# Earlier places in three queues: modulation tiles, a conv loop's product sums, a norm's centring and a table load

## The chip, the cores and the metric

The kernel runs on one core of a Trainium2 chip. A core has TensorE (matmuls; PE in the profile, its weight loads PEld), VectorE (DVE), ScalarE (ACT), GpSimd (POOL) and SyncE (SP), which here issues nearly all DMAs. Each engine works through its own queue in order, and engines wait for each other by semaphores. Three of the names below are memories: SBUF, which all engines read and write, PSUM, where TensorE accumulates and which VectorE and ScalarE read and write too, and HBM, where inputs and weights lie. The metric is device time in microseconds (us).

## The reference, cut to what matters

Three model blocks in a row on one sequence of 512 tokens with 1024 features, all in float32. The change touches the start of the first block and the middle of the second:

```python
# first block: six modulation vectors from a condition c of 1024 values
mod = silu(c) @ ada_w + ada_b                      # 1024 x 6144
sh_m, sc_m, g_m, sh_f, sc_f, g_f = split(mod, 6)
h = rms_norm(x, mix_norm_g) * (1.0 + sc_m) + sh_m  # wants the first 2048 columns of mod
proj = h @ w_in                                    # dq, dk, dv, sq, sk, sv, then attention
...
# second block, conv module: 2048 channels, 31 taps
a, b, z = split(h @ w_in, 3)
u = a * sigmoid(b)
c = causal_depthwise_conv(u, dw_w) + dw_b          # 31 multiply-adds for each channel
mu, var = mean(c), mean((c - mu) ** 2)             # over the 2048 channels
cn = (c - mu) * rsqrt(var + EPS) * ln_g + ln_b
y = silu(cn) * silu(z)
x = x + y @ w_out                                  # conv_out
...
# after it, retention: q and k are turned by angles positions * inv_freq
```

## The kernel before

Activations lie transposed: a chunk is 128 features on the partitions by 512 tokens. `st.X` holds the 8 chunks of x, `st.A` 32 chunks of work space, `st.spare` 16 more; `Hh`, `Hl` and `Bh`, `Bl` hold the high and low part of the 8 chunks that the next matmuls read. To keep float32's accuracy each product is made of three: high by high, high by low, low by high (line 1329).

**The weight stream** (`weights_part`). Weights come in tiles of 1024 rows by 256 columns (1 MB), alternately into the two slots of `st.raw`. SP loads a tile when GpSimd has split the tile before the last (lines 1215 to 1222); GpSimd splits it into `Wh` (line 1276) and `Wl` (line 1282, four instructions) once TensorE is through with the tile before the last; TensorE multiplies it in 48 matmuls, into one of two accumulators of two PSUM banks each; VectorE or ScalarE takes the result. The list that `program` makes fixes the order on each engine: segments of tiles, and between them parts with their own programs. A part's SP program stands in SP's queue between the loads of the segment ahead and those of the segment behind. A segment can carry `beside` (more work for GpSimd behind a tile's split) and `after` (more for VectorE behind a tile).

**The modulation** (`modulation_parts`). `ada_w` is cut in 24 tiles like the weights. The first 8 give the shift and gain that the first norm wants. SP loads them in turn into four slots: two are the two of `st.raw`, two lie in `st.spare`; tile n+4 waits until tile n is used. VectorE multiplies seven of them by silu(c) and adds them up over the rows in 8 instructions (lines 482 and 484), TensorE adds the partitions (line 458); tile 3 (`BY_PE`) TensorE multiplies itself, in 16 matmuls (line 469). The first two tiles of `w_in` can only be loaded when `raw` is free again. The other 16 tiles go through `st.spare` beside the projections. Before the third tile of `w_in`, SP issues 11 small loads (`beside_weights`: lambdas, head parameters, `skip` in single elements).

**The conv module** (`conv_module_steps`). Eight pairs of channel chunks, three weight tiles for each: sigmoid of b (ScalarE), the gated product (`glu`, VectorE, lines 2771 to 2774), silu of z (ScalarE). Of the 31 taps VectorE does 23, 46 multiply-adds a pair (line 2805); ScalarE starts the sums with two (line 2762) and makes the products of six more (line 2767), and GpSimd adds these six up: `add_half` adds the first three behind one split and the others behind the next (line 2791). It waits for the semaphore `products`, which ScalarE raises once for a pair, behind the sixth.

**The norm of the conv module** (`conv_norm_parts`, "norm5"). It centres in two steps. TensorE sums chunks 0 to 9 (line 2861), ScalarE makes their mean, the pivot, in `st.spare` (line 2890). The pivot is subtracted from 16 chunks: the first 5 by GpSimd (`BY_POOL`, line 2884), the last two and 5 to 13 by VectorE (line 2943). ScalarE squares each (line 2898), TensorE adds the squares up (line 2871) and finds the rest of the mean from chunks 10 to 15 (lines 2866 and 2876). VectorE makes variance (lines 2945 to 2955), then for chunks 0 to 7 subtracts the remaining offset (line 2957), scales (2925), multiplies by the gate `times` (2929; chunks 16 to 31 of `A`) and makes the low part (2933), with ScalarE's silu and high part between. Chunks 8 to 15 follow in groups of 3, 3 and 2 behind the first three tiles of the next segment (`second_half`, line 2973). `norm5.ready(k)` says that chunk k's low part is done.

**What follows.** The list reads `conv_in, norm5, rescaled(), conv_out[0], tables, conv_out[1]`: `conv_out[0]` multiplies norm chunks 0 to 7 with four weight tiles, `conv_out[1]` chunks 8 to 15 with four more. `tables` (`rotary_parts`) makes the rotary angles: SP waits for `memory_free`, then loads the positions into chunk 16 of `A` (line 1824); VectorE works on them in chunks 17 and 18. GpSimd's part of the norm sits in `behind_first_tile`: behind the split of `conv_out[0]`'s first tile the first additions of the last pair, behind the second tile's the other additions and the centring.

## Time and profile before

| | |
|---|---|
| median of 3 runs | 2705.58 us (2704.51 to 2707.02) |
| profiled execution | 2704.16 us, of which the span of the trace is 2702.0 us |
| granted TensorE clock, mean over the span | 0.968 of full |
| TensorE busy | 2530.6 us (94%) |
| GpSimd busy | 1542.3 us (57%) |
| VectorE busy | 1405.9 us (52%) |
| ScalarE busy | 646.8 us (24%) |
| HBM read | 227.86 MB, 85 GB/s over the span |

The span runs from the first to the last record; the 2.2 us beside it lie around it. Busy time leaves out waiting, and semaphore and DMA-issuing instructions. Two levels of TensorE's clock occur, 1.2 and 2.4 GHz, which the windows show as 0.50 and 1.00. In the time line, "x3" stands for three instructions in a row with their whole length, and the brackets give the engine's idle time before the first and what ended it. An engine's name with a q (SPq, POOLq) is its queue: issuing, waiting, draining.

### The profile page before, as it was taken

The page shows a single profiled execution, that of the slowest core. Times are in us where ns is not written, and L with a number is a line of the kernel's source. Part 1 is how long each engine was busy: PE and PEld are TensorE (multiplying, and loading weights), DVE is VectorE, ACT ScalarE, POOL GpSimd, SP SyncE. Part 2 cuts the span into 40 slices and gives each one's busy share as a digit, 9 for nine tenths or more (in the row PEclk, how much of TensorE's full clock was granted, in tenths as well). Part 3 has the DMA queues.
Part 4 walks back from the last instruction along what each step waited for, and adds up shares of the span by engine and source line. Part 5 has one row for each costly group of instructions (what it writes and reads, how often), then busy time and mean ns, then how long its engine had stood idle before and what let it go on. Part 6 is the DMA issues. An engine that isn't in the chain of part 4 may idle for free.

```text
span 2702.0 us, 32177 instructions
## 1 busy us (share of the span) xinstructions
PE 2530.6 (94%) x11690; PEld 2019.7 (75%) x11690; DVE 1405.9 (52%) x1944; ACT 646.8 (24%) x1045; POOL 1542.3 (57%) x1039
## 2 busy tenths in 40 slices
PE   6998999999989997699999998998998998999997
PEld 4885678888777774578977885866887786878775
DVE  6886552221489998848214336243356134535354
ACT  3106630110353343321022114132113212100001
POOL 2640266766688886267633754525762665666552
PEclk8999999999999999899999999999999999999998
DMA  8650022223322221122220222312331222223221
GB/s 268 217 164 1 32 78 94 93 94 94 102 71 78 92 83 56 35 94 94 93 78 32 98 91 62 94 33 63 94 94 32 78 93 78 78 93 93 93 72 42
DMA packets 231014, 231.36 MB, mean 86 GB/s; under 512 B 10011, under 2 KB 228860, under 8 KB 230780
## 3 DMA queue, kind: packets, MB, share of 16 engines
q1 hardware_dynamic: 228368, 228.87, 26.6%
q8 instruction: 63, 1.03, 0.2%
q10 hardware_dynamic: 2540, 1.11, 0.2%
q14 instruction: 43, 0.35, 0.0%
HBM read 227.86 MB, written 2.10 MB: 85 GB/s over the span
## 4 chain that ended last, share of the span: by engine, by line
PE 79%; DVE 7%; ACT 3%; DVEq 3%; POOLq 3%; issue 1%; DMA 1%; POOL 1%; ACTq 0%; SPq 0%
PE PS L1329 67%; PE PS L1185 2%; POOLq L2794 2%; PE PS L1902 1%; POOLq L1278 1%; PE PS L930 1%; POOL Wl L1282 1%; DMA raw<-in_ada_w 1%; DVE PS L2805 1%; PE PS L2104 1%; ACT spare L2767 1%; PE PS L2121 1%; PE PS L2871 1%; PE PS L1893 1%; DVEq L2700 0%
## 5 line engine op out<-in xcount | busy, mean ns | idle before, releaser
L1282 POOL TENSOR_TENSOR Wl<-raw,Wh 128x512 fp32r<-128x512 f32 (+2 forms) x768 | 1049.4, 1397 | 28.8 <-issue 7.3
L1276 POOL TENSOR_SCALAR Wh<-raw 128x2048 fp32r<-128x2048 f32 (+2 forms) x196 | 366.9, 1873 | 932.9 <-PE PS L1329 495.6
L1329 PE MATMUL PS<-Hh,Wh 128*128 128x512 f32 (+1 forms) x1976 | 784.6, 397 | 68.6 <-POOL Wl L1282 23.3
L1329 PE MATMUL PS<-Hl,Wh 128*128 128x512 f32 (+1 forms) x1976 | 778.2, 394 | 0.0
L1329 PE MATMUL PS<-Hh,Wl 128*128 128x512 f32 (+1 forms) x1976 | 778.0, 394 | 0.0
L1329 PEld LDWEIGHTS PS<-Hh,Wh 128*128 128x128 f32 (+1 forms) x1976 | 375.2, 190 | 164.5 <-issue 50.6
L1329 PEld LDWEIGHTS PS<-Hh,Wl 128*128 128x128 f32 (+1 forms) x1976 | 374.7, 190 | 81.7 <-issue 1.0
L1329 PEld LDWEIGHTS PS<-Hl,Wh 128*128 128x128 f32 (+1 forms) x1976 | 375.6, 190 | 78.9 <-issue 0.7
L1329 PE MATMUL PS<-Bh,Wh 128*128 128x512 f32 x688 | 272.4, 396 | 27.2 <-POOL Wl L1282 18.4
L1329 PE MATMUL PS<-Bl,Wh 128*128 128x512 f32 x688 | 270.9, 394 | 0.0
L1329 PE MATMUL PS<-Bh,Wl 128*128 128x512 f32 x688 | 270.9, 394 | 0.0
L2805 DVE SCALAR_TENSOR_TENSOR PS<-spare,PS 128x512 f32<-128x512 f32 x368 | 251.8, 750 | 9.8 <-ACT PS L2762 2.2
L1329 PEld LDWEIGHTS PS<-Bh,Wh 128*128 128x128 f32 x688 | 131.1, 191 | 59.3 <-POOL Wl L1282 18.9
L1329 PEld LDWEIGHTS PS<-Bh,Wl 128*128 128x128 f32 x688 | 131.0, 190 | 27.6
L1329 PEld LDWEIGHTS PS<-Bl,Wh 128*128 128x128 f32 x688 | 131.2, 191 | 27.1
L1329 PE MATMUL PS<-Wh,Hh 128*128 128x256 f32 x512 | 145.1, 283 | 0.0
L1329 PE MATMUL PS<-Wh,Hl 128*128 128x256 f32 x512 | 144.9, 283 | 0.0
L1329 PE MATMUL PS<-Wl,Hh 128*128 128x256 f32 x512 | 144.9, 283 | 0.0
L1413 DVE SCALAR_TENSOR_TENSOR X<-X,PS 128x512 f32<-128x512 f32 (+1 forms) x64 | 41.1, 682 | 194.9 <-PE PS L1329 194.9
L2695 DVE TENSOR_SCALAR A<-PS,params 128x512 f32 (+1 forms) x68 | 47.9, 745 | 143.8 <-PE PS L1329 143.4
L2697 DVE SCALAR_TENSOR_TENSOR A<-PS,params,A 128x510 f32 (+5 forms) x160 | 112.4, 744 | 14.7 <-issue 13.5
L1329 PEld LDWEIGHTS PS<-Wh,Hl 128*128 128x128 f32 x512 | 98.3, 192 | 0.1
(458 smaller groups left out, 2899.4 us busy)
## 6 DMA issues: line engine op xcount, KB each, us to landing
raw<-in_w_in SPq DMA_DIRECT2D x44, 1024.0 KB, 5.8
raw<-in_w_ff SPq DMA_DIRECT2D x32, 1024.0 KB, 5.3
raw<-in_conv_w_in SPq DMA_DIRECT2D x24, 1024.0 KB, 5.2
raw<-in_ret_w_in SPq DMA_DIRECT2D x24, 1024.0 KB, 5.1
spare<-in_ada_w SPq DMA_DIRECT2D x20, 1024.0 KB, 7.2
raw<-in_w_up SPq DMA_DIRECT2D x20, 1024.0 KB, 5.4
raw<-in_w_out SPq DMA_DIRECT2D x8, 1024.0 KB, 5.0
raw<-in_conv_w_out SPq DMA_DIRECT2D x8, 1024.0 KB, 4.9
```

The costliest lines, as they stand in the source:

```text
L930: pe.matmul(self.SUMSQ, ones, self.sq[c % 4], start=(c == 0 and not self.pre), stop=(c == KC - 1)).then_inc(self.summed, 1)
L1185: mm = pe.matmul(acc_of(0)[0:m, b, :], w[:, k, b * P:b * P + m], x[:, k, :], start=(k == 0 and n == 0), stop=(k == KC - 1 and n == 2))
L1276: pool.tensor_scalar(st.Wh[0:rows, slot, k, 0:g.width], st.raw_slot(slot)[0:rows, k, 0:g.width], 1.0, 1.0, ALU.mult, ALU.mult)
L1278: pool.drain()
L1282: ins = pool.tensor_tensor(st.Wl[0:rows, slot, k, 0:g.width], st.raw_slot(slot)[0:rows, k, 0:g.width], st.Wh[0:rows, slot, k, 0:g.width].b ...
L1329: mm = pe.matmul(out, lhs, rhs, start=(k == parts[0][0] and n == 0), stop=(k == parts[-1][0] and n == 2))
L1413: ins = e.scalar_tensor_tensor(x, x, x_scale, a, ALU.mult, ALU.add)
L1893: mm = pe.matmul(st.PS[:, n % 2, 0:S - b * P], st.A[:, 8 + 2 * h + d, b * P:(b + 1) * P], st.A[:, 2 * h + d, b * P:S], start=(d == 0), sto ...
L2695: ins = e.tensor_scalar(out[0:m, b, :], acc[0:m, b, :], w, None, ALU.mult)
L2697: ins = e.scalar_tensor_tensor(out[0:m, b, back:S], acc[0:m, b, 0:S - back], w, out[0:m, b, back:S], ALU.mult, ALU.add)
L2794: e.drain()
L2805: e.scalar_tensor_tensor(s, U[:, b, k:k + S], wts[:, k, b:b + 1], s, ALU.mult, ALU.add)
```

## The change

Four edits.

1. **Modulation.** All eight first tiles get buffers of their own: tiles 0 to 3 the four slots in `st.spare`, tiles 4 to 7 `before_h`, a new name for the memory of `Hh` and `Hl`, which the first norm fills later. SP issues all eight without a wait in between, and `raw` is free for `w_in` from the start. TensorE multiplies tiles 3 and 7 itself, VectorE the six others.
2. **Products.** ScalarE raises `products` behind each of the six; `add_half` waits for three before its first half and for six before its second.
3. **Norm.** GpSimd centres ten chunks instead of five, and does all its work for the norm and the last pair behind the split of `conv_out[0]`'s first tile. VectorE centres six. ScalarE writes the pivot twice, for GpSimd in `st.spare` and for VectorE in PSUM; offset, rstd and mean square move from `st.spare` to PSUM banks 3 to 6.
4. **Tables.** SP's load of the positions waits for `norm5.ready(2)` instead of `norm5.ready(15)`.

```diff
@@ modulation_parts
-    SLOT = lambda s: st.raw_slot(s) if s < 2 else LATER_SLOT(s - 2)
+    SLOT = lambda n: LATER_SLOT(n) if n < N else \
+        st.before_h[:, 4 * (n - N):4 * (n - N) + 4, :].rearrange("p c (h n) -> p (c h) n", h=2)
-    N, BY_PE = 4, 3
+    N, BY_PE = 4, (3, 7)
-    rounds, by_dve = first // N, [n for n in range(first) if n != BY_PE]
+    rounds, by_dve = 1, [n for n in range(first) if n not in BY_PE]
...
-        for n in range(first):
-            load(sp, SLOT(n % N), n % N, n // N, n * TW)
-        sp.wait_ge(free[0], rounds + 1)
-
-    def second_slot_free(sp):
-        sp.wait_ge(free[1], rounds + 1)
+        for n in range(N):
+            load(sp, SLOT(n), n, 0, n * TW)
+        for n in range(N, first):
+            sp.dma_start(SLOT(n), w[:, :, ds(n * TW, TW)]).then_inc(landed_h[n - N], 16)
...
-        for k in range(1, len(by_dve)):
-            mm = add_up(k)
-        mm.then_inc(by_pe, 1)
+        for k in range(1, len(by_dve) - 1):
+            add_up(k)
+        pe.wait_ge(landed_h[BY_PE[1] - N], 16)
+        product(BY_PE[1])
+        add_up(len(by_dve) - 1).then_inc(by_pe, 1)
@@ conv_module_steps
             for b in range(2):
                 ins = e.activation(PROD[k][:, b, :], U[:, b, k:k + S], ACT.Copy, scale=wts[:, k, b:b + 1])
-        ins.then_inc(products, 1)
+            ins.then_inc(products, 1)
...
     def add_half(e, pair, half):
+        e.wait_ge(products, pair * BESIDE + (half + 1) * (BESIDE // 2))
         if half == 0:
-            e.wait_ge(products, pair + 1)
             e.sem_inc(going, 1)
@@ conv_norm_parts
-    EARLY, BY_POOL, HALF, RING = 10, 5, 8, 5
+    EARLY, BY_POOL, HALF, RING = 10, 10, 8, 5
...
-    pivot, offset, rstd = st.spare[:, 7, :], st.spare[:, 14, :], st.spare[:, 15, :]
-    square_mean, logs = st.spare[:, 13, :], st.spare[:, 12, :]
+    pivot, logs = st.spare[:, 7, :], st.spare[:, 12, :]
+    pivot_v, offset, rstd, square_mean = (st.PS[:, k, :] for k in range(3, 7))
+    rest, rest_sq = st.spare[:, 14, :], st.spare[:, 13, :]
...
         act.activation(pivot, TOTAL, ACT.Copy, scale=1.0 / (EARLY * P)).then_inc(pivot_in, 1)
+        act.activation(pivot_v, TOTAL, ACT.Copy, scale=1.0 / (EARLY * P)).then_inc(pivot_in, 1)
...
-            dve.tensor_tensor(src[c], src[c], pivot, ALU.subtract).then_inc(centred_v, 1)
-        dve.drain()
-        dve.tensor_scalar(offset, pivot, float(14 * P - EARLY * P) / width, None, ALU.mult)
+            dve.tensor_tensor(src[c], src[c], pivot_v, ALU.subtract).then_inc(centred_v, 1)
+        dve.tensor_scalar(rest, pivot_v, float(14 * P - EARLY * P) / width, None, ALU.mult)
...
-        dve.tensor_tensor(logs, offset, offset, ALU.mult)
+        dve.tensor_tensor(rest_sq, rest, rest, ALU.mult)
+        dve.tensor_copy(offset, rest)
...
         if (i, p) == (0, 0):
             conv_in.first_sums(pool)
-        if (i, p) == (0, 1):
             conv_in.last_sums(pool)
             centre_by_pivot(pool)
@@ program
+        st.before_h = nc.alloc_sbuf_tensor_at("before_h", [P, 2 * KC, S], F32, offset=before_h)
...
-                nc, st, t, norm5.ready(15), lambda c: queries.act_ready(c) if c < 8 else keys.act_ready(c - 8))
+                nc, st, t, norm5.ready(2), lambda c: queries.act_ready(c) if c < 8 else keys.act_ready(c - 8))
```

On GpSimd, from the last pair's last split on. Each `Wh` and `Wl` pair is one weight tile: the last of the conv module, then the first and second of `conv_out[0]`. Before:

```order
L1276 TENSOR_SCALAR Wh<-raw 128x2048
L1282 TENSOR_TENSOR Wl<-raw,Wh 128x512 x4
L2791 TENSOR_TENSOR spare<-spare 128x1024 x2
L1276 TENSOR_SCALAR Wh<-raw 128x2048
L1282 TENSOR_TENSOR Wl<-raw,Wh 128x512 x4
L2791 TENSOR_TENSOR spare<-spare 128x1024
L2791 TENSOR_TENSOR spare<-spare,extra 128x1024
L2791 TENSOR_TENSOR spare<-spare,A 128x1024
L2884 TENSOR_TENSOR A<-A,spare 128x512 x5
```

and after:

```order
L1283 TENSOR_SCALAR Wh<-raw 128x2048
L1289 TENSOR_TENSOR Wl<-raw,Wh 128x512 x4
L2798 TENSOR_TENSOR spare<-spare 128x1024 x3
L2798 TENSOR_TENSOR spare<-spare,extra 128x1024
L2798 TENSOR_TENSOR spare<-spare,A 128x1024
L2892 TENSOR_TENSOR A<-A,spare 128x512 x10
L1283 TENSOR_SCALAR Wh<-raw 128x2048
L1289 TENSOR_TENSOR Wl<-raw,Wh 128x512 x4
```

The five additions of products stand together, ten subtractions follow in place of five, and the second tile's split comes behind them all.

On VectorE, behind the conv of the last pair, up to the first three scalings of norm5. Before:

```order
L2943 TENSOR_TENSOR A<-A,spare 128x512 x11
L2945 TENSOR_SCALAR spare<-spare 128x512
L2948 SCALAR_TENSOR_TENSOR spare<-PS,spare 128x512
L2950 TENSOR_TENSOR spare<-spare 128x512
L2953 SCALAR_TENSOR_TENSOR spare<-PS,spare 128x512
L2955 TENSOR_TENSOR spare<-spare 128x512
L2957 TENSOR_TENSOR A<-A,spare 128x512 x8
L2925 SCALAR_TENSOR_TENSOR A<-A,params,spare 128x512 x3
```

and after:

```order
L2952 TENSOR_TENSOR A<-A,PS 128x512 x6
L2953 TENSOR_SCALAR spare<-PS 128x512
L2956 SCALAR_TENSOR_TENSOR spare<-PS,spare 128x512
L2958 TENSOR_TENSOR spare<-spare 128x512
L2959 COPY PS<-spare 128x512
L2962 SCALAR_TENSOR_TENSOR PS<-PS,spare 128x512
L2964 TENSOR_TENSOR PS<-PS,spare 128x512
L2966 TENSOR_TENSOR A<-A,PS 128x512 x8
L2934 SCALAR_TENSOR_TENSOR A<-A,params,PS 128x512 x3
```

Five subtractions are gone, one copy is new, and pivot, offset and rstd are read from PSUM (`PS`).

On TensorE at the start, behind the transposes of x: partition sums of VectorE's tiles (four matmuls a tile), squares of the first norm (128x512), and its own product of a tile (16 matmuls from `small`). Before:

```order
L458 MATMUL PS<-squares,A 128x1 x4
L667 MATMUL PS<-A,squares 128x512 x4
L469 MATMUL PS<-small,spare 128x1 x16
L667 MATMUL PS<-A,squares 128x512 x4
L458 MATMUL PS<-squares,A 128x1 x24
```

and after:

```order
L457 MATMUL PS<-squares,A 128x1 x4
L674 MATMUL PS<-A,squares 128x512 x4
L464 MATMUL PS<-small,spare 128x1 x16
L674 MATMUL PS<-A,squares 128x512 x4
L457 MATMUL PS<-squares,A 128x1 x16
L464 MATMUL PS<-small,before_h 128x1 x16
L457 MATMUL PS<-squares,A 128x1 x4
```

One tile's sums are gone, and a second product stands ahead of the last tile's sums.

## Rows read from the trace of the kernel before

**Rows 1.** The page, part 1: busy us (share of the span) xinstructions.

```profile
PE 2530.6 (94%) x11690; PEld 2019.7 (75%) x11690; DVE 1405.9 (52%) x1944; ACT 646.8 (24%) x1045; POOL 1542.3 (57%) x1039
```

**Rows 2.** Waits of TensorE, 735 to 1160 us: engine, line, releaser: total us, times, longest.

```profile
PE PS L1329 <- POOL Wl L1282: 40.5, 12, 18.4
PE PS L1329 <- DVE Hl L2933: 13.6, 1, 13.6
```

**Rows 3.** The same view for SP's queue, 1085 to 1210 us.

```profile
SPq L1824 <- DVE Bl L2933: 89.1, 1, 89.1
```

**Rows 4.** The chain that ended last, 1137 to 1160 us: start, us, what.

```profile
1137.12 0.34 SPq L1824
...
1137.57 7.55 DMA raw<-in_conv_w_out
```

**Rows 5.** Timeline of TensorE, 1153 to 1166 us: start, us, instruction [idle before <- releaser].

```profile
1153.43 0.80 PE L1329 MATMUL PS<-Bh,Wh 128*128 128x512 f32 x1 [18.44 <-POOL Wl L1282]
...
1158.57 0.39 PE L1329 MATMUL PS<-Bh,Wh 128*128 128x512 f32 x1
...
1165.86 0.39 PE L1329 MATMUL PS<-Bh,Wl 128*128 128x512 f32 x1
```

**Rows 6.** Timeline of VectorE, 1061 to 1132 us.

```profile
1061.12 6.74 DVE L2943 TENSOR_TENSOR A<-A,spare 128x512 f32<-128x512 f32 x11
...
1075.66 0.69 DVE L2953 SCALAR_TENSOR_TENSOR spare<-PS,spare 128x512 f32<-128x512 f32 x1 [5.37 <-PE PS L2871]
...
1103.88 4.52 DVE L2973 TENSOR_TENSOR A<-A,spare 128x512 f32<-128x512 f32 x3
...
1122.43 1.89 DVE L2973 TENSOR_TENSOR A<-A,spare 128x512 f32<-128x512 f32 x3
...
1130.01 1.28 DVE L1413 SCALAR_TENSOR_TENSOR X<-X,PS 128x512 f32<-128x512 f32 x2
```

**Rows 7.** Timeline of GpSimd, 1055 to 1112 us.

```profile
1055.11 6.18 POOL L2884 TENSOR_TENSOR A<-A,spare 128x512 f32<-128x512 f32 x5 [0.24 <-issue]
1102.55 1.92 POOL L1276 TENSOR_SCALAR Wh<-raw 128x2048 fp32r<-128x2048 f32 x1 [41.26 <-issue]
1104.61 6.65 POOL L1282 TENSOR_TENSOR Wl<-raw,Wh 128x512 fp32r<-128x512 f32 x4
```

**Rows 8.** The chain: the norm's sums, first matmuls of conv_out, and TensorE from 1206 us.

```profile
1065.32 10.31 PE PS L2871 x24
...
1089.23 13.14 PE PS L1329 x48
...
1206.23 175.15 PE PS L1329 x1134
```

**Rows 9.** Windows of 2 us: length, busy (x) by engine, granted clock, DMA share, GB/s.

```profile
1052.00:1054.00 2.00, 0.00 (x0) 0.00 (x0) 1.96 (x3) 0.00 (x0) 1.86 (x2) 1.00 0.00 1
...
1056.00:1058.00 2.00, 0.91 (x1) 0.50 (x2) 1.93 (x4) 1.00 (x2) 2.00 (x3) 0.50 0.00 0
```

**Rows 10.** Timeline of ScalarE: products of the last pair, and the pivot.

```profile
1027.76 5.01 ACT L2767 ACTIVATE spare<-spare 128x512 f32<-128x512 f32 x8
...
1046.95 0.60 ACT L2890 ACTIVATE spare<-PS 128x512 f32<-128x512 f32 x1 [6.18 <-PE PS L2861]
```

**Rows 11.** VectorE in the conv loop: its waits, and its 368 multiply-adds (ns min/median/max).

```profile
DVE spare L2771 <- PE PS L1329: 1.8, 3, 0.8
...
L2805 DVE SCALAR_TENSOR_TENSOR PS<-spare,PS x368: 746/750/758, 764.8 to 1057.5; 128x512 f32<-128x512 f32 x184
```

**Rows 12.** Waits of GpSimd, 735 to 1160 us.

```profile
POOL spare L2791 <- ACT A L2767: 20.5, 8, 3.4
```

**Rows 13.** The start: TensorE's wait, GpSimd's, and a window (columns above).

```profile
80.98 0.50 PE L1329 MATMUL PS<-Hh,Wh 128*128 128x512 f32 x1 [1.17 <-POOL Wl L1282]
...
73.13 2.09 POOL L1276 TENSOR_SCALAR Wh<-raw 128x2048 fp32r<-128x2048 f32 x1 [13.35 <-DMA raw<-in_w_in]
...
60.00:66.00 6.00, 5.55 (x25) 4.25 (x24) 5.38 (x11) 2.17 (x3) 0.00 (x0) 1.00 0.04 0
```

More of the change, by code:

```diff
@@ L460, in add_up, with product @@
             return mm
+        def product(n):
+            for b in range(2):
+                for k in range(KC):
+                    mm = pe.matmul(column(n, b), SLOT(n)[:, k, b * P:(b + 1) * P], silu_c[:, k:k + 1],
+                                   start=(k == 0), stop=(k == KC - 1))
+            return mm
         pe.wait_ge(c_act, 1)
@@ L2871, in square @@
             pe.matmul(SUMSQ, st.ones, ring[k % RING], start=(k == 0), stop=(k == n - 1)).then_inc(added, 1)
-        for k in range(BY_POOL - 1):
+        for k in range(BY_POOL):
             square(k)
@@ L2877, in _ @@
         mm.then_inc(rest_summed, 1)
-        for k in range(BY_POOL - 1, n):
+        for k in range(BY_POOL, n):
             square(k)
@@ L3131, in first_steps @@
                 seg.beside_load = lambda sp, i, p, at=at: [load_later(sp, n) for n in beside[at + p]]
-            dq.beside_load = lambda sp, i, p: mod_products.second_slot_free(sp) if p == 0 else [load_later(sp, n) for n in beside[1]]
             rope_tables, rope, rope_done = rope_parts(nc, st, t, slot_read)
```

39 lines of the change are left out of this document (20 added, 19 removed).

## The prediction

> **What bounds the kernel now.** The page's busy times come first: TensorE is busy for 94% of the span [rows 1], so a change is worth what it takes from TensorE's idle time or from its half-clock time, and work saved on another engine is worth nothing until TensorE waits for it. The next view is therefore who TensorE waits for. In the stretch that holds the conv module, its norm and the first half of `conv_out` (735 to 1160 us), it waits 40.5 us in 12 places for GpSimd's weight split and once 13.6 us for the norm's first low half [rows 2]. The largest single piece, 18.4 us, is the one to look at closest. SP's own waits name its origin: SP stood 89.1 us at line 1824 [rows 3], where it is to load the positions for the rotary tables but first waits for `norm5.ready(15)`, the last of the norm's sixteen chunks. SP works in order, and the next weight tile, the fifth of `conv_out`, is behind that wait. The chain shows what followed: SP gets free at 1137.12, the tile lands 7.55 us after it is asked for at 1137.57 [rows 4], GpSimd splits it, TensorE starts at 1153.43, 18.44 us after it had ended the fourth tile [rows 5], at 1134.99.
>
> **The positions' wait, `ready(15)` to `ready(2)`.** The positions and their tables go into chunks 16 to 18 of `A`, which are the gates of norm chunks 0 to 2 alone, so the new wait ends some 3 us after the first matmul of `conv_out`. I call the start of that matmul M; it is 1089.23 before [rows 8]. What is late next? Four conditions stand before the fifth tile's matmuls, which want to start at M+45.8 (1134.99 less 1089.23). (1) Its load needs the raw slot, free when the third tile is split: M+22.0 (1104.61 and 6.65) [rows 7]; landing 7.6 us later, M+29.5. (2) Its split needs the third tile's matmuls done, M+35 (45.8 less one tile of 10.9; a tile is 48 matmuls at 0.228 us, below), and takes 8.7 us, what the row of the contended third tile says (1102.55 to 1111.26) [rows 7]: M+43.6, so 2 us to spare. (3) The accumulator needs VectorE's addition of the third tile, at 1130.01 and 1.28 long [rows 6], M+42.1, 3.7 us to spare. (4) The norm's chunks 8 to 15: the last came at 1137.1, where SP's wait ended [rows 4], or M+48, but are wanted at the end of the tile, 8 us after its start. So the whole wait goes: **-18.4 us**.
>
> The wait also costs on the far side. After it the first twelve matmuls take 1153.43 to 1158.57, 5.14 us; the 32 from there to 1165.86 take 7.29, 0.228 each, and twelve of these are 2.73 us [rows 5]. TensorE came back at the lower level, 1.2 GHz, after standing still. Without the wait it doesn't stand: **-2.4 us**. Behind it the chain lies on TensorE's own matmuls, 1134 of them in a row from 1206 to 1381 us [rows 8], so nothing there takes the gain back. VectorE's nine table operations move from TensorE's idle time to the time of tile five and stretch beside GpSimd's split (three chunks took 4.52 us beside it against 1.89 without it [rows 6], 1.1 us extra each where contended). At 1.5 us each, as in that group, they end about M+63, the addition of tile five (M+56.7) is some 6 us late, and its accumulator is free at about M+64, wanted only at M+67.6: nothing.
>
> **The norm.** Before, GpSimd subtracts the pivot from 5 chunks in 6.18 us, behind five additions of products and the split of `conv_out`'s second tile [rows 7], and VectorE from the other 11 in 6.74, once its last conv is done at 1061.12; the sum of squares is then ready at 1075.66 [rows 6], 14.5 us on. TensorE is what runs in between: 1065.32 to 1075.63, 24 matmuls for 12 squares, 0.86 us a square [rows 8]. The new order does ten chunks on GpSimd, before that split: the pivot is there at 1047.55 [rows 10], and ten at 1.236 us end by 1059.9, before VectorE is free. ScalarE's and TensorE's share for these ten runs along with them (about 0.6 and 0.86 us, both under 1.24). From VectorE's start there remain 0.7 us for its first subtraction, then two chunks for the late total and six squares, eight times 0.86 or 6.9 us, and 0.1 for the handing over: 7.7 against 14.5, **-6.8 us**. VectorE's six subtractions (6 at 0.61, 3.7 us) and the four operations for the offset behind them (at the same 0.6 us, 2.4 and their drains) fit under TensorE's 7.7. The extra ScalarE copy of the pivot (0.6) lies under GpSimd's first subtraction. GpSimd's split of tile two now comes behind them and ends near 1068, with TensorE wanting it at M+13: some 27 us of cover; beyond them every us later would be a us of TensorE's. From the squares to M the same operations follow, 13.6 us (1075.63 to 1089.23).
>
> Their operands are in PSUM now. In the trace an operation with a PSUM operand steps as fast as one without: 1.28 us for two additions from PSUM, 0.60 apart, and 6.74 for eleven SBUF subtractions, 0.605 apart [rows 6]; I count nothing. The Trainium skill says otherwise ("VectorE: DVE Perf Modes", the section on the TRN2 errata): a VectorE operation costs 58 cycles on top of its elements from SBUF and 120 from PSUM, which at its 0.96 GHz is an estimate of 0.065 us more for each, 1.1 us over the some 17 on the path; by it the norm's term would be 5.7. This trace does not agree.
>
> In the second half of the norm the PSUM operands save VectorE time where GpSimd splits beside it, up to 2.6 us for a group of three [rows 6], and the earlier wish for tile five costs some back. It is VectorE's slack, not TensorE's: nothing.
>
> **The conv loop's products.** GpSimd waits 8 times, 20.5 us together, for ScalarE's sixth product, of which it first needs three [rows 12]; three products are six activations of 0.61 us, 3.7 us [rows 10], so the longest, 3.4, goes too. But GpSimd does not set the loop's length. VectorE runs its 46 multiply-adds of each pair back to back and waits for TensorE 3 times, 1.8 us together [rows 11]; that is what a GpSimd that is 2.6 us earlier for each pair can give. About 0.1 us of each wait is the signal's way: **-1.5 us**, with 0 and 1.8 as ends.
>
> **The first modulation.** One of seven tiles goes from VectorE to TensorE, whose product runs while VectorE does the others, all loads go out unasked, and the first matmul of `dq` can come some 1 to 2 us earlier. But two tiles later TensorE waits 1.17 us for the third weight tile, at 80.98, because GpSimd waited 13.35 us for its DMA until 73.13; and that DMA came late because the queue moved nothing from 60 to 66 us, working off SP's small scattered loads behind the megabytes [rows 13]. The bytes ahead of these are the same before and after, and the queues were full before too. TensorE gets to that wait earlier and waits longer: **0**, with ends of 1.2 us lost (an equal delay of that tile) and 2 us gained (all that the norm gains, should the tile come earlier too).
>
> **The sum** is 18.4 + 2.4 + 6.8 + 1.5 + 0 = 29.1 us off the profiled execution's 2704.16 us (span 2702.0 and 2.2 around it): 2675.1. The median of the runs is 1.4 us above that execution, so 2676.5 for the median. Its own range is 2673 to 2680.
>
> **Rivals.** (a) *TensorE sums at half clock.* Before, it stood still for 5.8 us; the clock was still full 2 us into that and at half when it resumed [rows 9]. The new order also ends ten squares early: if TensorE is through with `conv_in` sooner, the pivot comes sooner, and it may stand over 4 us before VectorE's two late chunks. The first 5 us or so of the eight sums then go at half speed, 2.6 us lost: 2679. For it: TensorE's slack in the loop; against: the ten squares keep it at work for 70% of the time up to then. 0.13. (b) *PSUM operands cost as in the skill's rule*; as a mechanism of this kernel, VectorE's path after the squares is 1.1 us longer: 2677.6, 0.04. (c) *The gap closes but for the split.* The 2 us to spare of condition 2 is small: if VectorE's rows hold GpSimd up more than in the third tile's split, TensorE waits 2 to 5 us: about 2680.5, 0.08. (d) *The change doesn't do what it says:* SP gets past the positions only late, for a reason that the rows don't show, and 20.8 us stay: 2697, 0.05. (e) *The start gives its 2 us too:* 2674.5, 0.05. (f) *Slower:* VectorE's 368 multiply-adds set the conv loop, and in the new order GpSimd's additions fall on other ones of them and on ScalarE's writes. If they got 0.079 us longer each (29.1 over 368), the gain would be gone; at 0.1 us it is 2713. Against it: beside GpSimd or not, all 368 took 0.746 to 0.758 us [rows 11]. 0.03. My forecast has 0.62.
>
> **How the numbers follow.** Predicted is the likeliest case, 2676.5. The range takes in its own range, (a), (b), (c) and (e) with the ends of the start's term: 2670 to 2685; (d) and (f) are left out with 0.08, and the rest of two tenths is for sizes that I misjudge. A measurement of this kernel can tell about 0.2%, 5.4 us, from no change: faster by more than that 0.95 (all but (f), and a part of (d)), within it 0.02, slower 0.03.
>
> **What would show it.** Right: SP's wait at the positions ends some 3 us after `conv_out` begins; TensorE has no wait between its fourth and fifth tiles, and the granted clock stays full there; from VectorE's last conv to the first matmul of `conv_out` 21 us instead of 28; GpSimd's wait for products gone and VectorE's waits for TensorE in the loop with it; a wait at the third weight tile at the start of 2 to 3 us, ending near 81 us. Wrong: a new wait of TensorE for GpSimd at the fifth tile; half clock in the norm's sums; subtractions with the pivot in PSUM that step above 0.65 us; multiply-adds of the conv above 0.70 us.

## The result, and the profile after

| | before | changed |
|---|---|---|
| median of 3 runs | 2705.58 us | 2685.93 us (2683.37 to 2687.91) |
| ratio to before | | 0.9926, 95% interval 0.9904 to 0.9949 |
| span of the profiled execution | 2702.0 us | 2684.1 us |
| granted clock, mean over the span | 0.968 | 0.969 |

The change makes the kernel 19.7 us faster. 29.1 had been forecast; the time lies 0.9 us above the upper end of the range. Two more groups of runs gave medians of 2682.52 and 2684.34 us for the same kernel, 22.4 and 18.8 us under before: both inside the range, and both well above the 2676.5 that was called likeliest.

The answers to [rows 2] and [rows 3] come first: the changed kernel's waits of TensorE and of SP's queue (engine, line, releaser: total us, times, longest), 735 to 1160 us.

```profile
PE PS L1336 <- POOL Wl L1289: 17.9, 7, 3.6
PE PS L1336 <- DVE Hl L2942: 13.6, 1, 13.6
PE PS L1336 <- issue: 4.1, 1, 4.1
PE PS L2884 <- DVE A L2952: 2.3, 1, 2.3
...
SPq L1831 <- DVE Hl L2942: 22.7, 1, 22.7
```

The wait of 18.4 us is gone, and SP waits 22.7 us for the norm instead of 89.1. The fourth row is new: TensorE stood 2.3 us for VectorE's first late chunk. The chain through the same place (start, us, what), for [rows 8]:

```profile
1061.75 3.55 PE PS L2884 x4
1065.29 5.30 PE PS L2879 x12
...
1084.13 93.82 PE PS L1336 x402
1177.95 2.58 PE PS L863 x6
1180.53 175.15 PE PS L1336 x1134
```

All eight tiles of `conv_out` are now in one piece of 402 matmuls. From its start, M, to the 1134 matmuls it is 96.4 us, before 117.0 (1206.23 less 1089.23): 20.6 us gained, for 20.8 forecast. VectorE's timeline through the norm, for [rows 6]:

```profile
1061.00 3.67 DVE L2952 TENSOR_TENSOR A<-A,PS 128x512 f32<-128x512 f32 x6
...
1070.62 0.70 DVE L2962 SCALAR_TENSOR_TENSOR PS<-PS,spare 128x512 f32<-128x512 f32 x1 [3.19 <-PE PS L2879]
...
1110.05 1.88 DVE L2982 TENSOR_TENSOR A<-A,PS 128x512 f32<-128x512 f32 x3
...
1119.51 1.28 DVE L1420 SCALAR_TENSOR_TENSOR X<-X,PS 128x512 f32<-128x512 f32 x2 [0.18 <-PE PS L1336]
```

From VectorE's start to M it is 23.1 us, before 28.1: 5.0 gained, for 6.8. The sum of squares came 9.6 us after the start instead of 7.7. Windows of the same place (length, busy us and instructions (x) of PE, PEld, DVE, ACT, POOL, granted clock, DMA share, GB/s) show why:

```profile
1060.00:1062.00 2.00, 0.25 (x1) 0.26 (x2) 1.91 (x3) 0.28 (x1) 2.00 (x2) 1.00 0.00 0
1062.00:1064.00 2.00, 2.00 (x3) 0.72 (x3) 2.00 (x4) 2.00 (x4) 2.00 (x3) 0.50 0.00 0
```

TensorE was through with the ten squares at 1059.4 and stood still; it came back at 1.2 GHz. In the conv loop the distance from 736 us to VectorE's last conv shrank by 3.0 us, for 1.5; VectorE's waits for TensorE are gone. Of GpSimd's 20.5 us for products 14.1 stay, in 6 waits of up to 2.5.

So the middle gained 28.6 us: at 736 us the changed kernel is 2.9 us behind before, at the 1134 matmuls 25.7 ahead (1206.23 less 1180.53). At the end it is only 17.9 ahead. **7.8 us are lost behind 1206 us, in code that the change does not touch.** One of the places, the first matmul of the third block's w_in and the chain piece that it begins, of before and then of the changed kernel:

```profile
1673.49 0.50 PE L1329 MATMUL PS<-Hh,Wh 128*128 128x512 f32 x1 [1.76 <-DVEq L1257]
...
1673.49 68.14 PE PS L1329 x480
```

```profile
1651.28 0.50 PE L1336 MATMUL PS<-Hh,Wh 128*128 128x512 f32 x1 [1.81 <-DVEq L1264]
...
1651.28 69.74 PE PS L1336 x480
...
1653.40 0.63 PE L1336 MATMUL PS<-Hl,Wh 128*128 128x512 f32 x1
```

The stand of TensorE is nearly the same, 1.76 and 1.81 us; before, the clock stays up behind it. In the changed kernel the matmuls step 0.43 us apart from 1652.6 to 1655.5 us, at 1.2 GHz, and the piece is 1.6 us longer. This place belongs less to the change than it seems: e4 and e16 below, which are the kernel before with a later start, have the longer piece too (69.76 and 69.74 us). At another place, the second block's retention, TensorE stood 2.6 us before and 3.0 after, behind a load of `decay` that was 0.5 us longer. The window behind the stand, of before and then of the changed kernel:

```profile
1389.00:1392.00 3.00, 2.62 (x11) 1.65 (x10) 0.71 (x2) 0.00 (x0) 0.00 (x0) 1.00 0.86 280
```

```profile
1363.00:1366.00 3.00, 2.79 (x8) 2.27 (x8) 1.04 (x3) 0.00 (x0) 0.00 (x0) 0.50 0.70 227
```

### The profile page after: what moved, and what is told of

Its sections match the earlier page's. It is cut to its first block, busy times and chain, and to the rows that moved or that the text cites. A ratio compares the mean times of both kernels' runs of the same rounds, so it can differ in the third digit from the quotient of the medians.

```text
span 2684.1 us, 32215 instructions
## 1 busy us (share of the span) xinstructions
PE 2538.7 (95%) x11714; PEld 2026.8 (76%) x11714; DVE 1394.6 (52%) x1932; ACT 647.5 (24%) x1046; POOL 1546.5 (58%) x1044
## 4 chain that ended last, share of the span: by engine, by line
PE 76%; DVE 12%; DVEq 5%; SPq 2%; ACT 2%; issue 1%; DMA 1%; ACTq 0%; POOLq 0%; POOL 0%
PE PS L1336 64%; DVE PS L2812 7%; DVEq L2814 2%; PE PS L1192 2%; PE PS L1909 1%; SPq L431 1%; PE PS L937 1%; PE PS L2111 1%; PE PS L2128 1%; PE PS L1900 1%; DMA raw<-in_w_in 1%; SPq L438 0%; DVEq L2707 0%; PE PS L2472 0%; PE PS L1553 0%
## 5 line engine op out<-in xcount | busy, mean ns | idle before, releaser
L1336 PE MATMUL PS<-Hh,Wh 128*128 128x512 f32 (+1 forms) x1976 | 784.3, 397 | 66.5 <-POOL Wl L1289 20.4
L1336 PEld LDWEIGHTS PS<-Bl,Wh 128*128 128x128 f32 x688 | 130.6, 190 | 26.9
L2704 DVE SCALAR_TENSOR_TENSOR A<-PS,params,A 128x510 f32 (+5 forms) x160 | 112.3, 743 | 14.8 <-issue 13.6
```

The costliest lines, as they stand in the source:

```text
L1336: mm = pe.matmul(out, lhs, rhs, start=(k == parts[0][0] and n == 0), stop=(k == parts[-1][0] and n == 2))
L2704: ins = e.scalar_tensor_tensor(out[0:m, b, back:S], acc[0:m, b, 0:S - back], w, out[0:m, b, back:S], ALU.mult, ALU.add)
```

## The experiments

All medians are in us. "Behind" is how much later than in the profiled execution of before the same piece of the chain starts (minus: earlier), at the third weight tile (81), `conv_in` (736), the 1134 matmuls (1206) and the end of the span. The clock is the mean over the executions of the run.

| run | median | before beside it | ratio, 95% interval | clock | behind at 81, 736, 1206, end |
|---|---|---|---|---|---|
| changed | 2685.93 | 2705.58 | 0.9904 to 0.9949 | 0.970 | 0.1, 2.9, -25.7, -17.9 |
| e1 wait's edit alone | 2689.84 | 2704.11 | 0.9930 to 0.9960 | 0.9710 | 0.2, 2.8, -10.6, -13.8 |
| e2 no modulation edit | 2678.88 | 2704.11 | 0.9884 to 0.9914 | 0.9728 | 0.2, 2.5, -25.2, -24.2 |
| e3 changed, 4 memsets | 2684.94 | 2704.11 | 0.9919 to 0.9946 | 0.9702 | 3.9, 7.7, -21.9, -18.9 |
| e4 before, 4 memsets | 2706.27 | 2704.11 | 0.9998 to 1.0017 | 0.9679 | 2.7, 6.0, 6.5, 3.7 |
| e5 changed, again | 2682.52 | 2704.88 | 0.9914 to 0.9938 | 0.9712 | 0.5, 1.7, -26.9, -26.2 |
| e6 no norm edit | 2694.28 | 2704.88 | 0.9954 to 0.9980 | 0.9684 | 0.0, 2.8, -14.3, -13.3 |
| e7 no products edit | 2681.67 | 2704.88 | 0.9906 to 0.9931 | 0.9713 | 0.3, 2.9, -22.3, -20.8 |
| e8 e2, small loads late | 2676.43 | 2704.88 | 0.9879 to 0.9910 | 0.9735 | -1.2, -1.1, -28.9, -24.8 |
| e9 changed, third time | 2684.34 | 2703.17 | 0.9908 to 0.9935 | 0.9708 | 0.3, 1.5, -27.1, -19.5 |
| e10 e2 again | 2678.52 | 2703.17 | 0.9893 to 0.9920 | 0.9722 | 0.2, 2.4, -25.2, -24.3 |
| e11 modulation edit alone | 2710.41 | 2703.17 | 1.0016 to 1.0034 | 0.9655 | 0.3, 1.8, 1.8, 5.5 |
| e12 changed, small loads late | 2682.41 | 2703.17 | 0.9911 to 0.9939 | 0.9706 | -2.2, -0.8, -29.2, -24.8 |
| e13 e11, tile 7 on VectorE | 2702.55 | 2704.32 | 0.9989 to 1.0006 | 0.9686 | 0.3, 0.2, 0.2, -3.5 |
| e14 e11, 4 memsets | 2715.12 | 2704.32 | 1.0022 to 1.0050 | 0.9658 | 3.4, 7.4, 8.0, 15.1 |
| e15 before, 2 memsets | 2707.49 | 2704.32 | 1.0002 to 1.0019 | 0.9672 | 1.4, 4.7, 5.5, 5.4 |
| e16 before, 8 memsets | 2709.76 | 2704.32 | 1.0013 to 1.0032 | 0.9682 | 5.4, 8.8, 9.0, 5.4 |
| e17 e13 and an extra product | 2707.21 | 2704.14 | 1.0003 to 1.0028 | 0.9667 | 2.8, 2.9, 3.0, 2.6 |
| e18 changed, tile 7 on VectorE, small loads late | 2676.80 | 2704.14 | 0.9880 to 0.9918 | 0.9712 | -0.9, 0.7, -27.6, -26.2 |

### The wait alone, and all without the norm or the products

e1 is before with one edit, e6 and e7 are the changed kernel with one edit undone. Of e6 and e7 one line each is shown.

```diff
-                nc, st, t, norm5.ready(15), ...     (e1: this and nothing else)
+                nc, st, t, norm5.ready(2), ...
-    EARLY, BY_POOL, HALF, RING = 10, 10, 8, 5       (e6: the norm's edit undone)
+    EARLY, BY_POOL, HALF, RING = 10, 5, 8, 5
-            ins.then_inc(products, 1)               (e7: the products' edit undone)
+        ins.then_inc(products, 1)
```

> The kernel before with the fourth edit alone: SP waits for norm chunk 2 instead of chunk 15 before it loads the positions. The profile of the changed kernel shows TensorE without a wait between the fourth and fifth tiles of conv_out, so that term was right. Theory 1 (the local gains are as forecast; about 9 us went to stretches at 1.2 GHz at places whose code is unchanged): 20.8 us less here at the place itself, and the total off by up to 4 us to either side, since such stretches come and go when the time of everything behind moves. Theory 2 (the edit moves work that hits back later, in the retention and the third block): the retention's first matmuls slow down here just as in the changed kernel, some 3 us, and the total gains 15 to 18 us.

> The changed kernel without its edit of the norm: the norm is computed as before, the wait for the positions is the new one. Locally, from the first matmul of conv_out to the 1134 matmuls in a row: before 117.0 us, with all edits 96.4. If the norm's operands in PSUM are what took the last 6.5 us out of that stretch (the run with the wait's edit alone had 102.95), it is about 103 here, with a stand of TensorE of some 4 us before the fifth tile. From VectorE's last conv to that first matmul 28 us instead of 23. Total, if the far parts are as in the changed kernel: 2685.9 + 6.5 + 5.0 = 2697; if the losses behind 1206 us are only to be had with the changed kernel's times, 2690. The rival (the norm's edit gives nothing beyond its 5 us, the rest is chance): 96 to 98 locally, 2691.

> The changed kernel without its edit of the conv loop's products: GpSimd waits for all six products of ScalarE again. If the loop gained its 3.0 us (forecast 1.5) through this edit, VectorE has three waits for TensorE in the loop again and conv_in's stretch from 736 us to VectorE's last conv is 1.5 to 3.0 us longer; total 2687.5 to 2689. The rival (the loop's gain came from the other edits, since the shift at 736 us was +2.9 and is taken up by slack): the same stretch as with all edits, total 2684 to 2688.

From M to the 1134 matmuls e1 takes 102.95 us and e6 102.55, the changed kernel 96.4. A part of the gap stays in both. The chain of e1, and its rows of VectorE behind the third tile:

```profile
1092.69 45.81 PE PS L1329 x192
1138.50 4.02 issue
1142.52 50.54 PE PS L1329 x210
...
1127.91 5.75 DVE L2925 SCALAR_TENSOR_TENSOR A<-A,params,spare 128x512 f32<-128x512 f32 x3
1133.59 4.09 DVE L2929 TENSOR_TENSOR A<-A 128x512 f32<-128x512 f32 x3
1137.60 3.58 DVE L2933 SCALAR_TENSOR_TENSOR Bl<-A,Bh 128x512 fp32r<-128x512 f32 x3
1141.10 1.27 DVE L1413 SCALAR_TENSOR_TENSOR X<-X,PS 128x512 f32<-128x512 f32 x2
```

TensorE wants tile five at 1138.50 and starts 0.15 us behind the end of the third tile's addition. That addition began at M+48.4, in before at M+40.8. Before, GpSimd idled there, since tile five had not come, and these three groups took 2.08, 1.89 and 1.89 us. With the gap gone GpSimd splits beside them, and they take 5.75, 4.09 and 3.58. In the changed kernel two of VectorE's four operations for a chunk read one operand from PSUM, and beside the same splits they stay short: 1.88 us for three subtractions, where [rows 6] had 4.52. The Trainium skill states this ("SBUF — State Buffer", Who interferes with whom): a VectorE instruction with two SBUF inputs contends with a GpSimd instruction that reads SBUF, one with at most one does not, unless it runs in a 2-port perf mode. By it the move to PSUM pays just where GpSimd splits; for the norm's operations this trace agrees. One input is not enough for every operation, though: one of the table's `tensor_scalar` operations, with a single tensor from SBUF, took 0.43 us beside an idle GpSimd in before (L1840) and 1.35 beside the split in the changed kernel (L1847). The norm's edit is worth 11.8 us in the medians (e6 to e5), of which the profiles show some 5 before M and 6.2 from M to the 1134 matmuls. No run has the PSUM operands without the new order of the subtractions; behind M, though, the two kernels differ in these operands alone.

e7 has VectorE's three waits for TensorE back (2.8 us) and GpSimd's eight for products (20.4). From 736 us to VectorE's last conv it takes 325.4 us, e5 322.3: the loop's gain came through this edit. At M 2.8 us of the 3.1 are left. Its median is the same as e5's, though: 2.8 us are less than what the far part gives or takes.

### Is the loss behind 1206 us the same each time?

> The changed kernel once more, nothing left out. It asks whether its 2685.9 us, and the places behind 1206 us at which it lost about 8 us of its 26 us gain, belong to the kernel or to one run. Theory A (where TensorE's clock falls to its lower level, 1.2 GHz, behind a short stand depends on the kernel's times, and these are the same each time): median 2685 to 2687, the third conv block again some 4 to 5 us longer than before, the retention 3 us. Theory B (it falls now here, now there): the profile shows other places, and the median lies anywhere from 2679 to 2688.

> The changed kernel a third time, beside the other three of this group. At the start of the 1134 matmuls its two profiles are 25.7 and 26.9 us ahead of before, at the end 17.9 and 26.2: the first loses 8 us behind unchanged code, the second 0.7. Theory A (each execution draws its own short stretches at 1.2 GHz there): again 26 to 27 us ahead at the 1134 matmuls, and anything from 17 to 27 at the end; median 2681 to 2686. Theory B (the changed kernel as such loses there): a loss of 5 to 8 us behind 1206 us as in the first profile.

Of three profiles of one kernel, ahead by 25.7, 26.9 and 27.1 us at the 1134 matmuls, two lose 7.8 and 7.6 us behind it and one 0.7. The 14 timed executions lie between 2676.58 and 2687.91. So neither theory holds alone. One part of the loss is in all three: from the start of the 1134 matmuls to the 768 behind the retention (1445.34 us in before, 1422.68 in the changed kernel) before takes 239.1 us, and the three take 242.2, 243.0 and 242.3. Behind that the execution decides: from the third block's w_in to the end the three take 1032.8, 1025.1 and 1032.5 us, before 1028.5, and before with a later start 1024.9 to 1028.3. At the w_in place the twenty profiles of all kernels show how fine the difference is: the piece of 480 matmuls takes 68.1 to 68.2 us in the five with a stand of 1.76 to 1.78 us, 69.7 to 69.8 in the five with 1.80 to 1.82, and with 1.79 it is 68.1 to 68.2 in two and 69.7 to 69.8 in eight. How much goes with the clock is seen within before itself: of its 85 executions the 24 with a mean clock of at most 0.966 have a mean span of 2704.4 us, the 17 at 0.970 one of 2698.7.

### The modulation edit

e2 and e10 are one kernel, the changed one with the old modulation; e11 is before with the new one alone.

> The changed kernel with the modulation as it was before. In the changed kernel everything behind 110 us stood 1.8 to 2.9 us later than before. Theory 1a (the modulation edit causes it: GpSimd's split now begins before VectorE's norm and slows it, TensorE gets earlier to the third weight tile, stands 2.5 us and comes back at 1.2 GHz): the stretch to 400 us is 2.9 us shorter than in the changed kernel, and the total 2 to 5 us less (2682). Theory 2a (the start is the same with and without it; the 2.9 us are chance): total within 1.5 us of the changed kernel.

> The changed kernel without its modulation edit, again, beside the changed kernel on the same chip. Theory A (the modulation edit moves nothing that TensorE waits for; the 7.0 us between the two in an earlier group were chance, since the kernel with the wait's edit alone is 2.8 us behind before at 736 us as well and has the old modulation): the two agree within 2 us. Rival B (the edit costs time): the same 5 to 7 us less than the changed kernel, 2676 to 2679.

> The kernel before with the modulation edit alone. Theory A: the third weight tile's matmuls start within 0.5 us of before (80.98), total within 2 us of before, 2703 to 2707. Rival B (the edit costs 3 to 7 us, through TensorE's product at 1.2 GHz and the norm's slower operations beside GpSimd's earlier split): 2708 to 2712, with the first matmul of dq 1.3 us or more later than before. Rival C (it gives the time that it was meant to give): 2700 to 2703.

Without the edit the gain over the before beside it is 25.2 us in e2 and 24.7 in e10, where the changed kernel has 19.7 and, beside e10, 18.8: 5.6 and 5.8 us. The edit alone costs 7.2, and its interval excludes no change. Rival B stands, in size. Where it was expected, at the start, little is seen. Timelines of TensorE and VectorE of the changed kernel:

```profile
36.72 5.79 PE L464 MATMUL PS<-small,before_h 128*128 128x1 f32 x32
...
44.32 0.17 DVE L506 TENSOR_TENSOR mod<-PS,params 128x16 f32<-128x16 f32 x1 [5.39 <-PE PS L457]
...
45.28 5.63 DVE L706 SCALAR_TENSOR_TENSOR A<-X,mod,A 128x512 f32<-128x512 f32 x3
```

and of before:

```profile
24.45 3.73 PE L469 MATMUL PS<-small,spare 128*128 128x1 f32 x32
...
44.06 0.17 DVE L498 TENSOR_TENSOR mod<-PS,params 128x16 f32<-128x16 f32 x1 [1.55 <-PE PS L458]
...
44.57 5.05 DVE L699 SCALAR_TENSOR_TENSOR A<-X,mod,A 128x512 f32<-128x512 f32 x3
```

VectorE is through with its tiles 3.5 us earlier, but TensorE's product of tile 7 then stands in the way, at 1.2 GHz for most of its 5.8 us, and the modulation is ready 0.3 us later than before. TensorE has no stand ahead of it: it goes from the sums of 33.23 us straight into the product, and the granted clock falls to 0.5 near 38 us, in the middle of one-column matmuls. GpSimd's first split, 1.8 us earlier, stretches three of the norm's operations by 0.6. The first matmul of `dq` comes at 52.73 us, before at 51.44. The third weight tile starts at the same time as before, behind a wait of 2.52 us. With the old modulation e1 and e2 are 2.8 and 2.5 us late at 736 us as well, so the changed kernel's 2.9 us there are no sign of the edit: the profiled execution of before was quick.

e13 has the edit's loads and buffers, but VectorE sums tile 7; e17 is e13 with TensorE's 32 matmuls added, into columns that nothing reads.

```diff
-    rounds, by_dve = 1, [n for n in range(first) if n not in BY_PE]
+    rounds, by_dve = 1, [n for n in range(first) if n != BY_PE[0]]     (e13, e17, e18)
...
-        for k in range(1, len(by_dve) - 1):
-            add_up(k)
-        pe.wait_ge(landed_h[BY_PE[1] - N], 16)
-        product(BY_PE[1])
-        add_up(len(by_dve) - 1).then_inc(by_pe, 1)
+        for k in range(1, len(by_dve)):                                (e13, e18)
+            mm = add_up(k)
+        mm.then_inc(by_pe, 1)
...
+                pe.matmul(st.PS[:, 6, 60 + b:61 + b], SLOT(BY_PE[1])[:, k, b * P:(b + 1) * P], silu_c[:, k:k + 1],
+                          start=(k == 0), stop=(k == KC - 1))           (e17: ahead of the last add_up)
```

> The kernel before with the modulation's new loads and buffers alone: tile 7 is still summed by VectorE, not TensorE. The whole edit cost 6.5 us (11 executions), with the third weight tile no later in its profile and the product of span and mean granted clock unchanged (2615.0 against 2614.9 us), the clock 0.0024 lower. If TensorE's product of tile 7 brings that, this kernel is at 2703 to 2706 with a mean clock of 0.968; if the loads at once (or only the moment at which things happen) bring it, 2709 to 2711 at 0.9655. In its place: first matmul of dq some 1 to 2 us later than with the whole edit.

> The kernel of the modulation's loads alone (2702.6 us, mean clock 0.9686), and TensorE's 32 matmuls of tile 7 added at the place where the whole edit has them, into columns that nothing reads; VectorE still makes the sum that counts. Theory X (TensorE's 32 more matmuls there are what costs, wherever their result goes): 2709 to 2711 with a mean clock near 0.9655. Theory Y (it is VectorE's missing tile, with dq's first matmul and the norm's chunks moved against the rest, that sets other places for the clock's falls): 2702 to 2704 at 0.9685.

e13 takes 2702.55 us: the loads at once and their buffers cost nothing, and give nothing that can be told. The cost is tile 7 on TensorE, 7.9 us between the medians of e11 and e13 (9.0 with each against the before beside it). e17 lies between: 4.7 us over e13 in the medians, with the clock between theirs. But its profile has a delay of its own, since here TensorE does the product behind VectorE's last but one tile:

```profile
40.88 6.96 PE L481 MATMUL PS<-small,before_h 128*128 128x1 f32 x32
...
49.66 0.17 DVE L509 TENSOR_TENSOR mod<-PS,params 128x16 f32<-128x16 f32 x1 [6.58 <-PE PS L457]
```

and the third weight tile starts 2.8 us late. Between X and Y its median doesn't decide; what its profile says is told below.

### The start moved as a whole

```diff
+        for _ in range(4):                          (e3, e4, e14; 2 in e15, 8 in e16)
+            dve.memset(st.extra[:, 0, :], 0.0)
+            dve.drain()
+        dve.drain().then_inc(late, 1)               (SP's and ScalarE's first loads wait for late)
```

> The changed kernel, with its first loads held back by four memsets on VectorE (some 1.5 to 2.5 us), and nothing else changed: everything behind moves by that delay. Theory 1 (a short stand of TensorE costs a stretch at 1.2 GHz or not, depending on when it falls): the pieces between two stands keep their lengths, but the stretches at 1.2 GHz come at other places than in the changed kernel, and the total is the changed kernel's plus the delay, give or take 2 to 6 us. Rival (the stretches belong to the new order of work): the same stretches at the same places, and the total is the changed kernel's plus the delay within 1 us.

> The kernel before with the same delay of its first loads. Theory 1: the kernel before was itself a draw; its stretches at 1.2 GHz move too, and its total is not 2705.6 plus the delay but 2 to 6 us off, rather more than less, since before had none in the retention and at the third block's start. Rival: 2705.6 plus the delay within 1 us, with the same stretches.

> The modulation edit alone, and all of the start later by the four memsets that cost before 2.7 us at the third weight tile. Theory P (what the edit costs is where TensorE's stands fall, not work): another offset, another clock; the mean granted clock comes back towards 0.968, and with 2618 us of span times clock as in the delayed kernel before, the total is 2706 to 2709 in spite of the delay. Rival W (the edit makes TensorE run slower as such, wherever it falls): clock 0.9655 again and 2710.4 + 2.7 = 2713.

> The kernel before, all of the start later by two memsets, half of the 2.7 us. Theory P: with the same work the mean granted clock moves by some thousandths from offset to offset, and the total by up to 7 us beyond the 1.35 us: anything from 2700 to 2711. Rival W (only work counts): clock 0.968, total 2705.2.

> The kernel before, all of the start later by eight memsets, some 5.4 us. Theory P: as for the two memsets, another clock than 0.968 at one of the offsets, total anywhere from 2703 to 2715. Rival W: clock 0.968, total 2709.3.

The third weight tile comes 1.4, 2.7 and 5.4 us later for 2, 4 and 8 memsets, and before's median moves by 3.2, 2.2 and 5.4 us: about the delay, with up to 1.8 us beside it. The clock stays within 0.001 of before's, and with the modulation edit at 0.966, with a total that grows by 4.7. Theory P, that the moment alone sets the clock, falls; what the edit costs moves with it.

### Small loads behind the weight tiles

```diff
-                norm1, lam_part, mod_later, dq, beside_weights, columns, dk, dv, ...
+                norm1, mod_later, dq, columns, dk, beside_weights, dv, ..., sv[0], lam_part, rope[0],
```

> The changed kernel without its modulation edit (that run took 2678.9 us), and with the small scattered loads of the rope rows and the lambda put behind the second segment's weight tiles in the list of parts, so that no small load stands before the third weight tile. My account of the start is that this tile waits only for the queue that works off these small loads: GpSimd's wait for its DMA, which ended at 73.1 us, then ends some 6 to 10 us earlier, TensorE's wait of 1.2 us at 81 us is gone, and with it what it loses at 1.2 GHz behind it: 1.2 to 3 us, 2676 to 2678. The rival (the tile is late through the bytes ahead of it, not the small loads): the tile at 81 us as before and 2679; if the small loads are then late for the rope, a new wait at 128 to 175 us and 2680 to 2684.

> The changed kernel, with its modulation edit, and the small scattered loads of the rope rows and the lambda behind the second segment's weight tiles. Without the modulation edit this order of the parts began the third tile's matmuls at 79.8 instead of 81.1 us, and the total was 2676.4. If the small loads were what held that tile, and what hid any gain of the modulation edit, it starts at 79.8 us or earlier here, no wait of TensorE for that tile is left, and the total is 1 to 3 us under the changed kernel's. If the modulation edit costs time by itself (B), the total is 3 us or more above 2676.

> The changed kernel with tile 7 summed by VectorE and the small scattered loads behind the second segment's weight tiles; its new loads and buffers stay. With tile 7 on TensorE the same order took 2682.4 us, without the whole modulation edit 2676.4. If tile 7 on TensorE is the whole cost of the edit in this kernel too, 2675 to 2678 with a mean clock near 0.973; if the loads at once cost here, 2681 to 2684 near 0.971.

GpSimd's timeline of e8, for the third weight tile of [rows 13]:

```profile
68.37 1.91 POOL L1276 TENSOR_SCALAR Wh<-raw 128x2048 fp32r<-128x2048 f32 x1 [8.59 <-PE PS L1329]
```

The tile no longer waits for its DMA but for TensorE, and starts 4.8 us earlier than at 73.13. TensorE has no wait left there, and starts it 0.9 to 2.2 us earlier in e8, e12 and e18. Of the medians e8's is 2.5 and 2.1 us under e2's and e10's, within what their intervals leave open. e12 shows the edit's cost once more: 5.6 us over e18, the same kernel with tile 7 on VectorE. e8 and e18, at 0.9894 and 0.9899 of before, have lower medians than the changed kernel in any of its groups; they can't be told from each other, so with tile 7 on VectorE the old and the new loads are worth the same.

### Where the modulation edit's time lies

The profiles, sorted by what was changed, show the time lost between the 1134 matmuls and the end (the last two numbers of the table):

| | tile 7 on TensorE | tile 7 on VectorE |
|---|---|---|
| gap at tile five closed | changed 7.8, e3 3.0, e5 0.7, e7 1.5, e9 7.6, e12 4.4: mean 4.2 | e2 1.0, e8 4.1, e10 0.9, e18 1.4: mean 1.9 |
| 4 us of the gap left | e6 1.0 | e1 -3.2 |
| gap open | e11 3.7, e14 7.1: mean 5.4 | before 0, e4 -2.8, e13 -3.7, e15 -0.1, e16 -3.6: mean -2.0 |

e17, with the tile on both engines and the gap open, has -0.4. Each row shows more lost with tile 7 on TensorE, 1100 us and more behind the place where it is computed, but in the first row the two fields overlap; the edit's cost itself rests on the medians. In the right column 3.9 us more are lost with the gap closed than with it open.

One place can be named, the retention. Its first work waits for the load of `decay`, and the twenty profiles fall in two groups there. The load as the chain shows it, of before, the changed kernel, e11 and e13:

```profile
1382.58 5.05 DMA spare<-in_decay
...
1356.88 5.51 DMA spare<-in_decay
...
1384.40 5.61 DMA spare<-in_decay
...
1382.73 4.91 DMA spare<-in_decay
```

In the ten profiles in which TensorE makes a product of tile 7 (e17 among them, with 5.37) it took 5.37 to 7.24 us, and in each of them the DMA queue that carries instructions (q8, 63 pieces of 16 KB in every profile) moved one piece during the load. In the other ten it took 4.91 to 5.05, and that piece came 11 to 13 us after the load's start. What an edit at 37 us has to do with it is the length of TensorE's program: 11690 matmuls before, 11714 with tile 7 on TensorE, 11722 in e17, and the pieces of q8 come at other places. e13 and e17 differ in TensorE's program alone, and the piece moved. That the piece is what lengthens the load is the likeliest reading of twenty profiles; no run moves it and nothing else.

From the start of the 1134 matmuls to the 768 behind the retention the six profiles with the gap closed and tile 7 on TensorE take 241.1 to 243.0 us, the four with it on VectorE 239.1 to 240.4: on average 2.3 us, of the 6 that the edit costs. With the gap open e11 takes 239.6 and e14 241.5, and before, e4, e13, e15 and e16 239.1 to 239.2. Where the rest of the edit's cost lies is open.

## Why the prediction was off, point by point

- **The gap, -18.4 and -2.4: right in sum, 20.6 measured, but not by its own reason.** The four conditions were the right ones, and the numbered third was mis-sized: the addition of the third tile was taken from before at M+42.1, "3.7 us to spare", from rows in which GpSimd idled. With the gap closed GpSimd doesn't, and the addition alone would have come at M+49.7 and left 4.0 us of the gap and 1.2 GHz behind it (e1: 14.1 us gained, not 20.8). The PSUM operands took that away, which the prediction saw, with their 2.6 us for a group, and booked as "nothing". That the sum came out is luck in part.
- **The norm, -6.8: 5.0 measured.** Rival (a), given 0.13, is what happened: TensorE stood before the late chunks and summed at half clock, 1.9 us lost for the 2.6 worked out. By the rule of the Trainium skill ("VectorE: DVE Perf Modes", the section on the TRN2 errata) each PSUM operand would cost an estimated 0.065 us more, 1.1 us here. The trace does not agree with it: the six subtractions took 3.67 us, 0.60 apart, as from SBUF, and from the sum of squares to M it is 13.5 us, before 13.6.
- **The conv loop, -1.5: 3.0 measured, above the end of 1.8.** The waits of VectorE went, as said, and with the products' edit undone they are back (e7: 3.1 us at the last conv, 2.8 at M). The end had been read from the 1.8 us of one execution; e7 has 2.8 and e1 2.4 in the same three waits. GpSimd's waits for products were to go whole, and 14.1 of 20.5 us stayed: without an effect on VectorE, but not as forecast.
- **The start, 0: right at its place, wrong for the kernel. This is the term that failed.** The third tile starts at 81.1 us behind a wait of 2.5, as said. The first matmul of `dq` does not come 1 to 2 us earlier but 1.3 later: TensorE's product was put beside VectorE's work at no cost, where it is on the path, at 1.2 GHz. And the edit costs 5.6 to 7.2 us in the medians, some five times the end of 1.2. The prediction looked for its cost only up to the third weight tile. The runs show it behind 1206 us: 2.3 us at the retention, the rest not located.
- **"Nothing there takes the gain back": failed.** This was argued from TensorE's own matmuls from 1206 to 1381 us, which is so far right, for that piece takes 175.15 us in both kernels. Behind it lie 1300 us in which TensorE often stands for a short time, and they took something back even without the modulation edit: e2 and e10 gain 27.7 and 27.6 us between 736 and 1206 us in their profiles, and 25.2 and 24.7 in the medians. These gains are inside the range. The sum as measured: 28.6 us in the middle, for 29.1 forecast in all, less some 3 behind it and some 6 for the modulation edit, is 19.6. That the median fell just outside the range and not just inside is a matter of the execution: the other two groups lie inside.
- **Rivals (c), (d), (f)** didn't occur: no wait for the split at tile five, SP past the positions at 1087.74, and the loop's 368 multiply-adds take 0.750 us in the median, as in [rows 11].

## What to carry to other kernels

Slack that is read from rows beside an idle engine is gone once the change puts that engine to work: cost such rows at their contended length. Where TensorE has many short stands, a local gain is passed on only in part, and a change of 0.2% needs several executions and the kernel without one edit; the three profiled spans of the changed kernel alone lie up to 8.3 us apart (2675.8 to 2684.1). Work moved to TensorE is not free when another engine waits for what stands behind it, and a longer program also moves its instruction loads: look for the cost in the whole kernel, not only at the place of the edit.

## What was not expected of the hardware

The same code is followed by a stretch at 1.2 GHz in one execution and not in another: in e2 and e10, which are one kernel, stands of 1.79 and 1.77 us before the third block's w_in end in pieces of 69.73 and 68.16 us. Spans of one kernel differ by up to 10 us, the longer ones with the lower clock (before 2696.9 to 2707.1, mean clock 0.970 to 0.965). A 1 MB load took 5.37 to 7.24 us in the ten profiles in which a 16 KB piece of instructions was moved beside it, and 4.91 to 5.05 in the ten others. VectorE's subtraction of three chunks beside a GpSimd split takes 4.52 us with two SBUF inputs and 1.88 us with one in PSUM.
